# Hybrid HGRN2, short-convolution and MoE layer: a new order for the first tile and the masks, a product behind a later level, a conversion one turn sooner

## The chip, the cores and the metric

The kernel runs on one core of a Trainium2 chip. The metric is device time in microseconds (us) of one execution; the profile is of one further execution of the same program. TensorE is PE in all rows (PEld is its weight load), VectorE is DVE, ScalarE is ACT, GpSimd is POOL, and SP issues transfers.

## The reference, cut to what matters

There is one sequence of 1024 positions, 16 learned meta rows ahead of it, and 1024 channels.

```python
xn   = rmsnorm(h, norm_mix_g)                       # h: 1040 x 1024
proj = xn @ w_in                                    # q, f, i, g_out, B, C, v
# HGRN2, chunks of 128 tokens, 4 heads of 128x128 state:
o     = scores(q, k, decay) @ v + (q * exp(b)) @ state
state = exp(b_last) * state + (k * exp(b_last - b)).T @ v
h = h + concat(y_hgrn, y_conv) @ w_out
# top-8 of 64 experts, SwiGLU of width 256, in blocks of rows
h = h + moe_ffn(rmsnorm(h, norm_ffn_g), ...)
out = rmsnorm(h, norm_final_g)[16:]
```

## The kernel before

Three phases follow each other. `phase_front` holds the norm, the input projection, the HGRN2 chunks and the convolution, `phase_out_route` the output projection and the router, `phase_experts` the expert blocks and the last norm. Every engine has its own in-order program, and semaphores tie them. A product that must be precise is three matmuls: each operand is split into a high part (converted by ACT) and a low part (DVE subtracts the high part): high*high, high*low, low*high.

**First stage (0 to some 80 us).** The token tiles run through one pipeline of five steps. `root(c)` is Square with a sum, then Sqrt, on ACT; `recip` is on DVE; then ACT scales the rows (L582), PE turns the tile by 8 transposes (`turned(c)`, L379), DVE multiplies by the gain from PSUM (L778), ACT takes the high part (`high`, L548) and DVE the low part (`low`, L752). The order of tiles is `order`: the 16 meta rows first, then x0 to x7. `values(j)` (L368 to L370, 24 matmuls of 512 columns) multiplies tile j by the value columns `wi` of `w_in`. These 2 MB come in one transfer and are split in four pairs by ACT (L589) and DVE (L785), behind the third tile (`WI_AT = 2`). PE's program is turned(0), turned(1), turned(2), values(0), turned(3), values(1) and so on. POOL writes the constants and then fourteen `affine_select` masks (L286, L289); the masks are first read by the HGRN2 chunks. Behind the norm POOL starts the weight loop of the late columns (`load_late`, `store_late`: load a raw part, wait until ACT and DVE have split it, store the parts to DRAM).

**HGRN2 turns (182 to 447 us).** There are eight turns, one for each chunk, in pairs r = 0 and r = 1. PE's program mixes seven level products (`level(l)`, L465; level 0 is L457) with pieces of the late projections, which fill the time between levels (`BETWEEN`: three units of 512 columns from one level to the next). DVE prepares each level: `factors(l)` (L883, L884) multiplies the decays that ACT has exponentiated, `logs` (L876, L877) prepares a later level, `keep_scores` (L894) takes a level's scores over. After the diagonal scores (L906) stand three steps: `blast` (L910), QE = QE*QS (L911) and KE = KK*DK (L912, "end keys"). PE needs KE for a transpose behind level 6, and QE and all scores for the output product at the turn's end. POOL meanwhile works on the convolution, the last two of its products of a pair being L359.

**Experts (from some 750 us).** There are 65 items, one in each turn. Of each item the down matrix is split by ACT (`high_down`, L1783) and DVE (`low_down`, L1859), and then PE runs `down_rest` (L1722) and `down` (L1733 to L1735). ACT multiplies by the gates (L1802, L1806), and POOL adds the rows to `acc_rows` by two indirect transfers (`add_rows`, L1629 and L1633), after a wait until the previous item's adds have landed and two small index copies (L1624). When the last add has landed, SP loads the accumulated rows and the final norm runs.

## Time and profile before

| | |
|---|---|
| three runs | 1652.81, 1654.74, 1662.01 us, median 1654.74 |
| the profiled execution | 1652.65 us, of which the span from first to last instruction is 1651.1 |
| mean granted clock of TensorE | 0.981 of full |
| PE busy | 1562.9 us (95%), 10204 matmuls |
| DVE, ACT, POOL busy | 754.2, 654.2, 660.6 us |
| transfers | 375.17 MB, 227 GB/s over the span |

A row of the timeline has the start, the duration, the engine, the line, the operation with output and input names, how many instructions are merged in it, and in brackets how long the engine sat idle before it and what ended that. A wait row says which instruction waited for which, how long in total, how often, and the longest. On an engine that is busy without a gap, a shorter wait elsewhere changes nothing; a gap of PE that is removed moves all behind it.

### The profile page before, as it was taken

How to read it: one execution, taken by the hardware profiler on the slowest of the kernel's cores; microseconds unless marked ns; L12 is line 12 of the kernel's file. 1: busy time of each engine (PE TensorE's matmuls, PEld its weight loads, DVE VectorE, ACT ScalarE, POOL GpSimd, SP SyncE). 2: the span in 40 equal slices, each digit the busy share in tenths (PEclk: the TensorE clock that was granted, in tenths of full speed). 3: DMA queues.
4: the chain of work that ended last, by engine and by line, in shares of the span. 5: the costliest groups of instructions: out<-in, count | busy, mean ns of one | idle time of the engine just before them, and what ended most of it. 6: DMA issues, size and time to landing. Idle time of an engine off the chain costs nothing.

```text
span 1651.1 us, 30076 instructions
## 1 busy us (share of the span) xinstructions
PE 1562.9 (95%) x10204; PEld 1344.5 (81%) x10204; DVE 754.2 (46%) x1536; ACT 654.2 (40%) x1054; POOL 660.6 (40%) x825
## 2 busy tenths in 40 slices
PE   5999999999889999889999999999999999999991
PEld 4789989889644666679999999999999999999980
DVE  3323777788688774423333333333333333333333
ACT  7334544444433312024444444444444444444443
POOL 3022245162403232424545444555444445555531
PEclk9999999999999999989999999999999999999995
DMA  5389321211160112369999999999999999999977
GB/s 180 97 269 311 133 77 51 76 51 52 62 251 27 39 52 80 129 223 320 330 316 325 328 320 326 327 324 323 321 326 325 323 327 322 328 313 329 322 219 235
DMA packets 100728, 375.17 MB, mean 227 GB/s; under 512 B 14943, under 2 KB 31904, under 8 KB 79694
## 3 DMA queue, kind: packets, MB, share of 16 engines
q1 hardware_dynamic: 60606, 246.60, 40.9%
q0 software_dynamic: 40080, 128.04, 28.8%
q8 instruction: 23, 0.38, 0.1%
q14 instruction: 19, 0.16, 0.0%
HBM read 300.68 MB, written 73.91 MB: 227 GB/s over the span
## 4 chain that ended last, share of the span: by engine, by line
PE 54%; DMA 1%; ACT 0%; DVE 0%; issue 0%; SPq 0%; POOLq 0%; ACTq 0%
PE gu L1711 34%; PE ype L1733 4%; PE yrest L1722 4%; PE ype L1734 4%; PE ype L1735 4%; PE xp L1692 3%; PE xp L1699 1%; DMA A<-acc_rows 1%; DMA acc_rows<-YE,sia 0%; DVE WL L1859 0%; ACT WH L1783 0%; DVE A L1896 0%; SPq L1589 0%; ACT junkf L1846 0%; ACT XS L1787 0%
## 5 line engine op out<-in xcount | busy, mean ns | idle before, releaser
L1711 PE MATMUL gu<-XS,place 128*128 128x160 f32 x4160 | 588.2, 300 | 0.7 <-ACT XS L1791 0.7
L1711 PEld LDWEIGHTS gu<-XS,place 128*128 128x128 f32 x4160 | 575.6, 190 | 6.2 <-ACT XS L1791 1.1
L1859 DVE TENSOR_TENSOR WL<-place,WH 128x2048 fp32r<-128x2048 f32 x65 | 149.2, 2295 | 320.1 <-ACT WH L1783 320.1
L1796 ACT ACTIVATE SS<-gu 128x160 f32<-128x160 f32 x130 | 39.5, 304 | 367.0 <-PE gu L1711 367.0
L1864 DVE TENSOR_TENSOR SS<-SS,gu 128x160 f32<-128x160 f32 x130 | 41.3, 318 | 257.3 <-ACT SS L1796 257.3
L1806 ACT ACTIVATE YE<-ype,gta 128x512 f32<-128x512 f32 x130 | 89.5, 689 | 111.4 <-PE ype L1735 111.4
L1097 POOL DMA_INDIRECT slot_table<-pay,si x64 | 63.2, 988 | 172.3 <-DVEq L1396 155.2
L1629 POOL DMA_INDIRECT acc_rows<-YF,sib x65 | 104.3, 1604 | 64.9 <-POOL sib L1624 55.0
L1615 POOL COPY gta<-tables 128x1 f32 (+1 forms) x65 | 124.0, 1907 | 8.2 <-POOLq L952 8.2
L1783 ACT ACTIVATE WH<-place 128x2048 fp32r<-128x2048 f32 x65 | 123.5, 1900 | 0.7 <-issue 0.7
L1633 POOL DMA_INDIRECT acc_rows<-YE,sia x65 | 108.5, 1669 | 27.1 <-issue 22.5
L1733 PE MATMUL ype<-WH,hidh 128*128 128x512 f32 x260 | 110.0, 423 | 0.0
L1734 PE MATMUL ype<-WL,hidh 128*128 128x512 f32 x260 | 103.3, 397 | 0.0
L1735 PE MATMUL ype<-WH,hidr 128*128 128x512 f32 x260 | 101.9, 392 | 0.0
L1602 POOL DMA_INDIRECT wi<-xn_rows,gi x64 | 65.1, 1018 | 53.2 <-POOL gi L1599 52.1
L1624 POOL COPY sia<-tables 128x1 int32 (+1 forms) x65 | 11.9, 184 | 173.0 <-DMA acc_rows<-YE,sia 171.2
L1787 ACT COPY XS<-xp 128x512 f32<-128x512 f32 x130 | 69.8, 589 | 26.7 <-PE xp L1692 18.2
L1733 PEld LDWEIGHTS ype<-WH,hidh 128*128 128x128 f32 x260 | 49.1, 189 | 36.3 <-issue 27.2
L1722 PE MATMUL yrest<-place,HF 128*32 128x256 f32 x1040 | 70.5, 389 | 5.2 <-DVE WL L1859 5.2
L1692 PE MATMUL xp<-ident,wi 128*128 128x128 f32 x520 | 67.4, 273 | 2.3 <-PEq L952 2.3
L465 PEld LDWEIGHTS sc<-wi 128*128 128x128 f32 x448 | 56.8, 192 | 13.1 <-issue 8.7
L368 PE MATMUL bank<-xT_high,wf_parts 128*128 128x384 f32 (+2 forms) x192 | 67.2, 350 | 0.0
(311 smaller groups left out, 2850.5 us busy)
## 6 DMA issues: line engine op xcount, KB each, us to landing
place<-in_w_gate_e SPq DMA_DIRECT2D x65, 1024.0 KB
place<-in_w_up_e SPq DMA_DIRECT2D x65, 1024.0 KB
place<-in_w_down_e SPq DMA_DIRECT2D x65, 1024.0 KB
place<-in_w_in POOLq DMA_DIRECT2D x16, 512.0 KB, 6.9
late_parts<-wq_parts POOLq DMA_DIRECT2D x8, 1024.0 KB, 5.9
late_parts<-xn_parts POOLq DMA_DIRECT2D x8, 1024.0 KB, 6.1
wf_parts<-late_parts POOLq DMA_DIRECT2D x8, 1024.0 KB, 5.0
w_low<-late_parts POOLq DMA_DIRECT2D x8, 1024.0 KB, 5.1
```

What stands on the lines that cost most here:

```text
L1615: last = pool.tensor_copy(gt[q][r][:, :], K.gate[r][:, bass.ds(n, 1)])
L1629: pool.indirect_dma_start(acc_q, bass.IndirectOffsetOnAxis(ap=si[q][1][:, :], axis=0), YF[q][:, :], None, compute_op=ALU.add).then_inc(s_a ...
L1633: pool.indirect_dma_start(acc_d, bass.IndirectOffsetOnAxis(ap=si[q][0][:, :], axis=0), YE[q][:, :], None, compute_op=ALU.add).then_inc(s_a ...
L1692: last = pe.transpose(xp[t // 4][:, t % 4, :], rows[:, t, :], K.ident[:, :])
L1711: last = pe.matmul(gu[f][:, k, :], raw[:, t, f * P:f * P + P], XS[:, q, t, :], start=(t == 0), stop=(t == KT - 1))
L1722: last = pe.matmul(yr[j * CAP1:(j + 1) * CAP1, :], HF[q][:, f, P:CAP], raw[:, f, j * DQ:(j + 1) * DQ], start=(f == 0), stop=(f == 1), tile ...
L1733: pe.matmul(yp[g][:, :], hh, high[:, f, cols], start=(f == 0), stop=False)
L1734: pe.matmul(yp[g][:, :], hh, low[:, f, cols], start=False, stop=False)
L1735: last = pe.matmul(yp[g][:, :], hl, high[:, f, cols], start=False, stop=(f == 1))
L1783: act.activation(WH[q][:, :], WR[q][2][:, :], ACT.Copy).then_inc(s_dhi, 1)
L1806: act.activation(YE[q][:, 512 * g:512 * g + 512], yp[g][:, :], ACT.Copy, scale=gt[q][0][:, 0:1]).then_inc(s_ya, 1)
L1859: tt(WL[q][:, :], WR[q][2][:, :], WH[q][:, :].bitcast(F32), ALU.subtract).then_inc(s_dlo, 1)
```

## The change

1. SP loads x0, the gain and the meta rows, then `wi` in two halves with a semaphore each, then x1 to x7.
2. The meta rows come last (`order = list(range(TT + 1))`). ACT runs one Sqrt on a constant before the first tile. It converts two pairs of `wi` behind tile 0's scaling and two behind tile 1's. PE runs `turned(1)` in the middle of `values(0)`, and later tiles are turned two ahead of the values, not three. DVE follows that order.
3. POOL's masks are written behind the norm, after the first two `load_late` and the blank rows.
4. In each HGRN2 turn KE is behind level l = 2, `blast` and QE at l = 6.
5. In `add_rows` the index copies stand ahead of the wait for the previous adds. The last item's `high_down` moves into the turn before it, behind that turn's first sigmoid.

The diff, cut:

```diff
-        order = [TT] + list(range(TT))
+        order = list(range(TT + 1))
@@ sync
+            load_x(0)
+            sp.dma_start(gmix[:, :], ...).then_inc(s_m, 16)
             sp.dma_start(xt[0:META, TT, :], ins["meta_tokens"]).then_inc(s_m, 16)
-            load_x(0)
-            load_x(1)
-            sp.dma_start(K.wi[:, :, :], w_in[:, :, COL_I:COL_I + HW]).then_inc(s_wi, 16)
-            for j in range(2, TT):
+            for k in range(2):
+                sp.dma_start(K.wi[:, 4 * k:4 * k + 4, :], ...).then_inc(s_wi[k], 16)
+            for j in range(1, TT):
                 load_x(j)
@@ tensor, values(j)
-                pe.wait_ge(s_lo, TT + 1 if j == TT else j + 2)
+                pe.wait_ge(s_lo, j + 1)
...
+                    if j == 0 and t == KT // 2 - 1:
+                        turned(1)
...
-            for c in range(3):
-                turned(c)
+            turned(0)
             for j in range(TT):
                 values(j)
-                if j + 3 <= TT:
-                    turned(j + 3)
+                if j + 2 <= TT:
+                    turned(j + 2)
@@ scalar
+            act.activation(rstd[:, TT + 1:TT + 2], K.eps[:, 0:1], ACT.Sqrt)
+            root(0)
+            scaled(0)
+            act.wait_ge(s_wi[0], 16)
+            values_high(0)
+            values_high(1)
+            high(0)
+            root(1)
+            scaled(1)
+            act.wait_ge(s_wi[1], 16)
+            values_high(2)
+            values_high(3)
+            root(2)
@@ vector, front
+            keep_turned(0)
+            values_low(0)
+            low(0)
+            recip(1)
+            values_low(1)
+            values_low(2)
+            keep_turned(1)
+            values_low(3)
+            recip(2)
@@ vector, turn
-                dve.wait_ge(s_ee, i + 2)
-                step(nc.vector.tensor_copy(blast...))
-                tt(QE[:, :, :], QE[:, :, :], QS[:, :, :], ALU.mult)
-                step(tt(KE[:, :, :], KK[:, :, :], DK[:, :, :], ALU.mult))
-                dve.sem_inc(s_ke, 1)
                 for l in range(1, NL):
...
+                    if l == 2:
+                        dve.wait_ge(s_ee, i + 2)
+                        step(tt(KE[:, :, :], KK[:, :, :], DK[:, :, :], ALU.mult))
+                        dve.sem_inc(s_ke, 1)
+                    if l == NL - 1:
+                        step(nc.vector.tensor_copy(blast...))
+                        tt(QE[:, :, :], QE[:, :, :], QS[:, :, :], ALU.mult)
@@ gpsimd, add_rows
+                for r in two:
+                    pool.tensor_copy(si[q][r][:, :], ...).then_inc(s_si, 1)
                 if not isinstance(n, int) or n > 0:
                     pool.wait_ge(s_ad, n * 32)
                     pool.sem_inc(s_free, 1)
-                for r in two:
-                    pool.tensor_copy(si[q][r][:, :], ...).then_inc(s_si, 1)
@@ scalar, experts, turn_
-                high_down(q, n, i + 1)
                 if ahead >= 1:
+                    high_down(q, n, i + 1)
                     sigmoid(0, n + 1)
+                if ahead == 1:
+                    high_down(1 - q, n + 1, i + 2)
```

ACT's queue from the start of the program. Before (`place` holds the token tiles, `xT_high` the turned tile's high part; 16x1024 is the meta tile):

```order
L538 ACT_TABLE_LOAD
L538 ACTIVATE place,ss<-place 16x1024
L541 ACT_TABLE_LOAD
L541 ACTIVATE rstd<-ss,eps 16x1
L538 ACTIVATE place,ss<-place 128x1024
L541 ACTIVATE rstd<-ss,eps 128x1
L582 ACTIVATE place<-place,rstd 16x1024
L538 ACTIVATE place,ss<-place 128x1024
```

The same queue in the change, from its start to the first high part:

```order
L587 ACT_TABLE_LOAD
L587 ACTIVATE rstd<-eps 128x1
L538 ACTIVATE place,ss<-place 128x1024
L541 ACTIVATE rstd<-ss,eps 128x1
L579 ACTIVATE place<-place,rstd 128x1024
L584 ACTIVATE wi_high<-wi 128x1024 x2
L548 ACTIVATE xT_high<-xn 128x8x128
```

The meta tile and one table load have left the head of the queue, and half of the value weights stands between tile 0's scaling and its high part, where all four pairs stood behind tile 1's high part.

DVE's queue in an HGRN2 turn, from the diagonal scores on. Before:

```order
L906 TENSOR_TENSOR SCT<-sc,ident 128x512
L50 REGISTER_ALU
L909 REGISTER_ALU
L910 COPY blast<-place 128x4
L50 REGISTER_ALU
L911 TENSOR_TENSOR place<-place 128x512
L912 TENSOR_TENSOR place<-place 128x512
L50 REGISTER_ALU
L882 REGISTER_ALU
L883 TENSOR_TENSOR wi<-wi,place 128x8x32
L884 TENSOR_TENSOR wi<-wi,place 128x8x32
```

In the change, from the same place:

```order
L934 TENSOR_TENSOR SCT<-sc,ident 128x512
L50 REGISTER_ALU
L910 REGISTER_ALU
L911 TENSOR_TENSOR wi<-wi,place 128x8x32
L912 TENSOR_TENSOR wi<-wi,place 128x8x32
L904 TENSOR_TENSOR wi<-place 128x32x8
L905 TENSOR_TENSOR wi<-place 128x32x8
L917 REGISTER_ALU
L922 COPY_PREDICATED SCT<-masks,sc 128x4x64
```

The factors of the next level (8x32) now follow the diagonal scores at once; the end keys' product stands behind the level after it.

ACT's queue at the end of the experts, from the last but one turn's down matrix. Before:

```order
L1783 ACTIVATE WH<-place 128x2048
L1796 ACTIVATE SS<-gu 128x160 x2
L1802 ACTIVATE YF<-yrest,gtb 128x256
L1805 REGISTER_ALU
L1806 ACTIVATE YE<-ype,gta 128x512
L1805 REGISTER_ALU
L1806 ACTIVATE YE<-ype,gta 128x512
L1781 ISA
L1782 REGISTER_ALU
L1783 ACTIVATE WH<-place 128x2048
```

In the change:

```order
L1813 ACTIVATE WH<-place 128x2048
L1826 ACTIVATE SS<-gu 128x160
L1812 REGISTER_ALU
L1813 ACTIVATE WH<-place 128x2048
L1826 ACTIVATE SS<-gu 128x160
L1832 ACTIVATE YF<-yrest,gtb 128x256
```

The last item's conversion stands between the two sigmoids, ahead of the previous item's three evictions.

## Rows read from the trace of the kernel before

**Rows 1.** Waits of PE, whole span: total, times, longest.

```profile
PE sc L465 <- DVE wi L884: 8.8, 5, 2.2
```

**Rows 2.** Timeline of the first 35 us, ACT, DVE and PE.

```profile
11.07 1.13 ACT L582 ACTIVATE place<-place,rstd 128x1024 f32<-128x1024 f32 x1
...
14.26 0.69 DVE L778 TENSOR_TENSOR xn<-kt_ps,gmix 128x512 f32<-128x512 f32 x1 [1.54 <-PE o_ps L379]
14.38 1.06 ACT L538 ACTIVATE place<-place 128x1024 f32<-128x1024 f32 x1 [1.98 <-DMA place<-in_x]
...
15.89 0.16 DVE L745 RECIPROCAL rstd<-rstd 128x1 f32<-128x1 f32 x1 [0.34 <-ACT rstd L541]
...
16.95 1.97 PE L379 MATMUL sc<-ident,place 128*128 128x128 f32 x8 [2.73 <-ACT place L582]
17.75 3.88 ACT L589 ACTIVATE wi_high<-wi 128x1024 fp32r<-128x1024 f32 x4
...
20.22 4.62 DVE L785 TENSOR_TENSOR wi_low<-wi,wi_high 128x1024 fp32r<-128x1024 f32 x4
...
21.58 0.77 PE L368 MATMUL bank<-wi_high,xT_high 128*128 128x512 f32 x1 [2.65 <-DVE wi_low L785]
...
29.34 0.48 PE L368 MATMUL bank<-wi_high,xT_high 128*128 128x512 f32 x1
...
34.98 1.06 PE L379 MATMUL sc<-ident,place 128*128 128x128 f32 x8
```

**Rows 3.** Transfers: size, us from issue to landing; x0's issue, then wi's.

```profile
place<-in_x SPq DMA_DIRECT2D x1, 512.0 KB, 3.3
...
wi<-in_w_in SPq DMA_DIRECT2D x1, 2048.0 KB, 10.2
```

**Rows 4.** POOL busy while it writes the masks, 2 to 17 us.

```profile
2.00:17.00 15.00, 14.36 (x17) 1.00 0.94 355
```

**Rows 5.** Timeline: the first store of the late parts, and the third conversion.

```profile
84.33 0.59 POOL L304 DMA_DIRECT2D late_parts<-wq_parts  x1 [17.31 <-DVE wq_parts L764]
...
96.14 1.06 ACT L571 ACTIVATE wq_parts<-place 128x1024 fp32r<-128x1024 f32 x1
```

**Rows 6.** Timeline of the second turn of a pair, DVE, POOL and PE.

```profile
219.75 0.68 DVE L906 TENSOR_TENSOR SCT<-sc,ident 128x512 f32<-128x512 f32 x1
...
221.38 2.99 POOL L359 TENSOR_TENSOR place<-place 128x512 f32<-128x512 f32 x2
221.39 1.87 DVE L912 TENSOR_TENSOR place<-place 128x512 f32<-128x512 f32 x1
...
225.12 1.38 PE L465 MATMUL sc<-wi 128*128 128x64 f32 x8 [2.16 <-DVE wi L884]
```

**Rows 7.** Stretch of two us behind that wait: all engines, then granted clock.

```profile
226.00:228.00 2.00, 2.00 (x7) 1.71 (x7) 1.53 (x6) 0.00 (x0) 0.00 (x0) 0.50 0.00 0
```

**Rows 8.** Timeline of the last items: SP's issues, ACT, DVE, PE and POOL.

```profile
1579.02 13.66 SPq L1566 DMA_DIRECT2D place<-in_w_down_e  x2
...
1599.40 0.30 ACT L1796 ACTIVATE SS<-gu 128x160 f32<-128x160 f32 x1 [1.86 <-PE gu L1711]
...
1605.17 0.29 DVE L1870 TENSOR_TENSOR hidr<-HF,hidh 128x128 fp32r<-128x128 f32 x1
...
1608.28 1.90 ACT L1783 ACTIVATE WH<-place 128x2048 fp32r<-128x2048 f32 x1
...
1610.21 2.29 DVE L1859 TENSOR_TENSOR WL<-place,WH 128x2048 fp32r<-128x2048 f32 x1 [4.75 <-ACT WH L1783]
...
1612.84 1.93 PE L1722 MATMUL yrest<-place,HF 128*32 128x256 f32 x16 [5.18 <-DVE WL L1859]
...
1615.99 0.19 POOL L1624 COPY sia<-tables 128x1 int32 x1 [5.18 <-DMA acc_rows<-YE,sia]
...
1617.25 1.57 POOL L1629 DMA_INDIRECT acc_rows<-YF,sib  x1 [0.95 <-POOL sib L1624]
```

**Rows 9.** Chain that ended last, in order of time: start, us, step.

```profile
1620.95 6.12 DMA acc_rows<-YE,sia
```

More of the change, by code:

```diff
@@ L177, in phase_front @@
         s_x = [sem(f"x_in{j}") for j in range(4)]
-        s_m, s_wi = sem("meta_and_gmix_in"), sem("wi_in")
+        s_m, s_wi = sem("meta_and_gmix_in"), [sem(f"wi_in{i}") for i in range(2)]
         s_c0, s_c = sem("consts_cleared"), sem("consts_set")
@@ L571, in late_high, with scaled @@
                 act.activation(duo[k % 2][:, 0, :], raws[k % 2], ACT.Copy).then_inc(s_ph, 1)
-            act.wait_ge(s_c, 3)
-            root(0)
-            for c in range(TT + 1):
-                if c < TT:
-                    root(c + 1)
+            def scaled(c):
                 j, n = order[c], rows_of(c)
```

82 lines of the change are left out of this document (42 added, 40 removed).

## The prediction

> **What bounds the kernel now.** I read the busy shares first: PE is busy for 95% of the span, so only its gaps and what lies behind its last matmul can be won. The waits of PE show which gaps touch this change. Five waits on DVE's factors in the HGRN2 turns sum to 8.8 us [rows 1]; one of 2.65 stands before the first value product and one of 5.18 before the last item's down product [rows 2, 8]. Between the value products and the turns the timeline shows PE without a gap, so what is won in the first stage reaches the turns whole, if the queues beside PE keep up. The end is different: the last add of rows starts at 1620.95 and takes 6.12 [rows 9], and all behind it (SP's loads, the last norm) is untouched. A gain at the end must come through that add.
>
> **Part 1, the first tile.** Before, value tile 1 starts at 29.34 and ends at 34.98 [rows 2], 5.64 us for 24 matmuls, 0.235 each. By 34.98 PE has turned the meta tile and x0 to x2 and has done values 0 and 1. I work out when it has done the same in the new order.
> - x0's transfer lands 3.3 us after its issue [rows 3]. It is now the first, issued at 1.0 (0.9 sooner), so it lands at 4.3. ACT's one table load is over by then: it needs only the constants of POOL. From the start of a Square to the end of the reciprocal are 15.89 + 0.16 - 14.38 = 1.67 us; scaling takes 1.13 and turning by a PE that has just begun 1.97 [rows 2]. So: reciprocal 6.0, scaled 7.2, turned 9.2, and with two gain products (0.69 each, overlapping) stored at 10.5.
> - The first half of `wi`: all 2 MB land in 10.2 us, with x0 and x1 ahead [rows 3]. With x0 alone ahead I estimate 8.0 for the first half, 10.5 for the second, 12.0 for x1. A pair costs ACT 3.88/4 = 0.97 and DVE 4.62/4 = 1.15 [rows 2]. ACT has two pairs by 10.0 and the high part of x0 by 11.6; DVE runs pair 0's low part to 11.7 and x0's to 12.9. Values 0 start at 13.0, not 21.58.
> - They don't run through. x1's norm starts at 12.0, is scaled at 14.9, and pairs 2 and 3 are high at 15.9 and 16.9. DVE: low pair 1 to 14.9, pair 2 to 17.1, then x1's gain products behind its turning (18.1 to 19.4), then pair 3 to 20.6. PE reaches pair 3 at 19.5, waits 1.1 and ends values 0 at 22.0. x2 is scaled only after the reciprocal behind pair 3 (ACT 20.8 to 21.9), its turning ends at 23.1, x1's high part at 23.0 and low part at 24.3: PE waits 1.2 more, runs values 1, and ends at 24.3 + 5.6 = 29.9.
>
> The meta tile's turning is still owed, half a us. Gain: 34.98 - 29.9 - 0.5 = **4.6**. After that a tile's chain within one values group is 1.3 + 1.06 + 1.15 and three hand-overs, some 4.4 of 5.64 us, so two tiles ahead is enough. Bounds: 2.2, if all of values 0 runs at the slow pace (24 x 0.1 more: a turning takes 1.97 at 16.95 and 1.06 at 34.98 [rows 2], so both paces exist here); 6.9, if both waits vanish.
>
> The table load: only 1.3 us lie on the old chain for each of two loads, and the new one lies beside x0's transfer. The Trainium skill, "ScalarE: Activation LUTs", section "What ACT_TABLE_LOAD costs", states about 2.66 us for each switch of sets, 1.38 of it a drain. By that the old chain would show a longer gap than it does, and the new load would end near 4.6, 0.3 behind x0's landing; the sum would be 4.3 in place of 4.6.
>
> **The masks.** They take POOL 14.4 us [rows 4]; nothing of the first stage reads them, so there they cost and give nothing. Now they stand between the blank rows (over at about 66, an estimate) and the first store of late parts. That store starts at 84.33, when DVE has the parts [rows 5]; moved 4.6 earlier it would want 79.7, and the masks end at 66.2 + 14.7 = 80.9. Queued behind are the store and the next raw load, about 1.3 us late. ACT wants that load at 96.14 - 4.6 = 91.5 [rows 5]; issued by 82.4 it is there at 89.4, if its 512 KB take 7 us, midway between 3.3 and 10.2 [rows 3]. Cost nothing, with 2 us of cover.
>
> **Part 2, the end keys.** In the second turn of each pair the diagonal scores end at 220.43. Then DVE runs blast, QE and KE, KE in 1.87 us since it stands against POOL's L359 [rows 6], and PE idles 2.16 before level 2. PE was ready at 225.12 - 2.16 = 222.96. In the new order the factors start at about 220.6 and end by 221.4, before level 2 is wanted, so this wait goes in all four second turns. They hold four of the five waits of rows 1, at 2.1 each 8.5 us; the fifth, 0.2, stands before the last level of all. Behind the first of them the granted clock is 0.50, the lower level (1.2 GHz), for two us and more [rows 7], after a PE that had idled 2.16: that costs 1.6 and goes too. What is late next: L359 lasts to 224.37 [rows 6] and now stands against the two logs. KE lost 1.2 to it, so I take 2.3 lost in all; scores and factors of level 3 are then over between 226.2 and 226.8, and PE, three units of 9 x 0.235 and a level further, wants them at 226.0. Wait 0.6. KE then adds 0.9 to the next round and QE 0.9 to the last, where DVE's round (3.1) is about PE's (3.0): another 0.4 in small waits. So 1.0 comes back in each of three turns. The fourth has no gate work in it and loses only 0.4 at its end, where QE stands before the last scores. Sum: 8.5 + 0.2 + 1.6 - 3.0 - 0.4 = **6.9**. Bounds: 3, if half of each wait comes back and the clock falls again; 10.3, if none does. PE's own wait for KE (behind level 6) has 10 us of cover. In the first turn of a pair PE waits for nothing and the sum of DVE's work is the same: nothing.
>
> The Trainium skill, "SBUF — State Buffer", section "SBUF: two separate sides", has the port pair of DVE and GpSimd as an exclusive lock: an operation with two SBUF inputs waits until the other's ends. KE's 1.87 agrees. By the lock each of L359's two products holds up one DVE instruction, which is the later end of my 226.2 to 226.8 and would make the sum 6.3.
>
> **Part 3, the end.** The last item's down matrix is issued by 1592.7, 7 us before its conversion can start at 1599.7, behind the sigmoid [rows 8]. ACT has it at 1601.6, before the second sigmoid. DVE subtracts behind its hidden products, from 1605.5 to 1607.8. PE ends the previous item at 1612.84 - 5.18 = 1607.7 and runs L1722 from 1608.1, not 1612.84 [rows 8]: 4.7 sooner, and at the fast pace. That does not reach the end. The last item's adds wait until the previous item's have landed, at 1615.99 [rows 8], and those are untouched. Today L1629 runs 1.26 behind that landing, the two copies in between, then L1633 waits for ACT until 1620.95 [rows 9]. Now ACT is done by 1613, the copies are made, L1629 starts at about 1616.6, takes 1.57, and L1633 starts at 1618.5, not 1620.95. I take 0.2 off, since a second add that starts sooner behind the first takes longer to land. Gain **2.2**. Bounds: 1.3 (L1629 where it is today, the landing 0.5 longer) and 2.9. In the other turns add_rows has slack and gives nothing.
>
> **Sum**, against the profiled execution: 1652.65 - 4.6 - 6.9 - 2.2 = 1638.9. It lies 2.1 below the median of three runs; I put the forecast between, at **1639.5**.
>
> **Rivals.**
> A. *The waits of the turns only move.* L359 meets the new order badly in each pair, and level 3 or 4 waits as level 2 did. For it: DVE's round is as long as PE's. Against it: DVE arrives 3 us earlier. Part 2 falls to 3: 1643.
> B. *PE runs slow in the first stage*, with short waits between short runs of matmuls. Part 1 falls to 2.2: 1642.
> C. *Something beside PE holds the turns' start in place.* DVE's split of the last late parts and their stores depend on PE's evictions, which speaks against it. Part 1 falls to 0: 1644.
> D. *Slower.* The masks on POOL run beside DVE's splits and stretch. KE's factor against POOL is 1.87/0.69 = 2.7; by that they'd take 39 us and end at 105, the raw load would land at 113, and ACT, in order, would hold PE's evictions from 91.5 on: PE loses about 17: 1639 + 17 = 1656. It decides from masks of 19 us (first wait); for slower by 0.5% they must take 44. Against it: they ran at their price beside DVE's splits of the first stage.
> E. *The early conversion does not run early*, the matrix not landed at 1599.7: if it holds the second sigmoid, which is due when PE ends its next product, part 3 is 0 or a loss of 2: 1641 to 1643.
>
> **How the numbers follow.** Forecast 0.60; A 0.16, B 0.08, C 0.07, D 0.03, E 0.06. The upper bounds of all parts together give 1632.6, the lower 1646.2. The range is 1634 to 1646.5. About 0.5% is what a measurement of this kernel can tell from no change, 8.3 us: faster needs 1646.5 or less. Same holds where two of A, B, C meet (0.09); slower is D (0.03); faster 0.88.
>
> **What would show it.** Values 0 start near 13 and values 1 end near 30, with two PE waits of about 1; the masks end near 81 and ACT's third conversion has no new wait; no PE wait of 2 us before level 2, no stretch at clock 0.50, small ones before level 3; L1722's last wait under 1 us, L1629 starting within a us of the landing, L1633 2 us sooner against the previous landing. I would be wrong most if x1's transfer lands after 14, or if the new waits in the turns exceed 1 us each.

## The result, and the profile of the changed kernel

| | before | after |
|---|---|---|
| median, this measurement | 1660.77 us (1652.81 to 1662.01, 5 runs) | 1643.35 us (1643.14 to 1645.78, 5 runs) |
| profiled execution, span | 1652.65 us, 1651.1 us | 1643.35 us, 1641.8 us |
| granted TensorE clock, mean of the span | 0.981 | 0.983 |

The ratio of the times is 0.9917, 95% interval 0.9895 to 0.9939. Measured twice more on other occasions, the changed kernel gave 0.9917 [0.9893, 0.9941] and 0.9928 [0.9906, 0.995]. So it is faster by 0.8%, and more than the 0.5% that can be told from no change. The forecast of 1639.5 was 3.9 us too low; the measured time lies inside the stated range. Between the two profiled executions 9.3 us were gained, where 13.7 were worked out.

Where PE waits now, longest first (PE's operation and line, what it waited for, us in total, times, longest); it answers to [rows 1]:

```profile
PE sc L378 <- ACT place L579: 7.8, 1, 7.8
PE xp L1722 <- PEq L982: 6.0, 1, 6.0
PE op L1167 <- DVE place L1362: 5.9, 1, 5.9
...
PE sc L465 <- DVE wi L912: 3.1, 6, 1.0
```

The factors' waits (`sc L465`) fell from 8.8 to 3.1 us. The second line has nothing to do with any edit: PE's own sequencer (PEq) waited 6.0 us at the barrier ahead of the experts, where all engines meet, and 2.3 in the kernel before.

The first stage, from the timelines (start, duration, engine, line, operation, idle before and what ended it), answers to [rows 2]; ACT, DVE and PE in the order of time:

```profile
1.03 1.28 ACT L587 ACT_TABLE_LOAD   x1 [1.03 <-PEq L1963]
2.33 0.20 ACT L587 ACTIVATE rstd<-eps 128x1 f32<-128x1 f32 x1
7.75 1.94 PE L378 MATMUL sc<-ident,place 128*128 128x128 f32 x8 [7.75 <-ACT place L579]
8.99 2.00 ACT L584 ACTIVATE wi_high<-wi 128x1024 fp32r<-128x1024 f32 x2 [1.38 <-DMA wi<-in_w_in]
12.22 1.23 DVE L767 TENSOR_TENSOR xT_low<-xn,xT_high 128x1024 fp32r<-128x1024 f32 x1
13.50 0.79 PE L367 MATMUL bank<-wi_high,xT_high 128*128 128x512 f32 x1 [3.81 <-DVE xT_low L767]
...
21.36 0.51 PE L367 MATMUL bank<-wi_high,xT_high 128*128 128x512 f32 x1 [1.11 <-DVE wi_low L796]
24.83 0.50 PE L367 MATMUL bank<-wi_high,xT_high 128*128 128x512 f32 x1 [0.90 <-DVE xT_low L767]
30.50 0.60 PE L378 MATMUL kt_ps<-ident,place 128*128 128x128 f32 x4
62.90 1.05 PE L378 MATMUL sc<-ident,place 16*128 16x16 f32 x8
```

Values 0 start at 13.50, values 1 end at 30.50 (34.98 before), and the meta tile's eight transposes cost 1.05 us at 62.90. Further on, three stretches are counted off by PE's first product of the turns, the first of the output stage behind them (`ms`) and the first expert product (`gu`):

```profile
179.17 1.15 PE L457 MATMUL sc<-place 128*128 128x128 f32 x8 [1.41 <-ACT place L694]
...
439.92 2.93 PE L1153 MATMUL ms<-place,ones 128*128 128x512 f32 x3 [2.87 <-ACT place L1286]
...
709.45 2.77 PE L1741 MATMUL gu<-XS,place 128*128 128x160 f32 x9 [0.74 <-ACT XS L1821]
```

In the kernel before the same three stand at 182.36, 449.64 and 716.40. So 3.2 us were won ahead of the turns; the turns took 260.75 in place of 267.28, 6.5 won; and the stretch from there to the experts took 269.5 in place of 266.8, 2.8 lost.

The end, which answers to [rows 8, 9] (PE's last down product and POOL's last two adds, from the timelines, and the landing, from the chain of waits):

```profile
1600.54 1.07 PE L1752 MATMUL yrest<-place,HF 128*32 128x256 f32 x16 [0.25 <-DVE WL L1891]
...
1609.34 1.57 POOL L1659 DMA_INDIRECT acc_rows<-YF,sib  x1 [5.44 <-issue]
1611.21 1.54 POOL L1663 DMA_INDIRECT acc_rows<-YE,sia  x1 [0.30 <-issue]
```

```profile
1611.21 6.52 DMA acc_rows<-YE,sia
```

The last add starts 14.94 us behind the down product of the item before it (at 1596.27), where it was 17.31 (1603.64 and 1620.95): 2.4 won. The landing took 6.52 for 6.12 and the experts 0.4 less, which cancel. Sum: 3.2 + 6.5 - 2.8 + 2.4 = 9.3, the whole difference of the two executions.

So three questions are open: is the loss of 2.8 ahead of the experts the change's doing; which edit carries what; and why do the times differ by more than the 9.3 of the two profiles? By the ratio it is 13.7; the two medians of five lie 17.4 apart, and the later sets, with 24 and 17 runs of the kernel before, give 13.6 and 12.4.

### The profile page after: what moved, and what is told of

Read it like the earlier page. It is cut to its first block, busy times and chain, and to the rows that moved or that the text cites. A ratio compares the mean times of both kernels' runs of the same rounds, so it can differ in the third digit from the quotient of the medians.

```text
span 1641.8 us, 30075 instructions
## 1 busy us (share of the span) xinstructions
PE 1557.7 (95%) x10204; PEld 1340.5 (82%) x10204; DVE 759.8 (46%) x1536; ACT 653.5 (40%) x1054; POOL 668.0 (41%) x825
## 4 chain that ended last, share of the span: by engine, by line
PE 54%; DMA 1%; DVE 1%; issue 0%; ACT 0%; POOL 0%; POOLq 0%; ACTq 0%; DVEq 0%; SPq 0%
PE gu L1741 35%; PE ype L1763 4%; PE yrest L1752 4%; PE ype L1764 4%; PE xp L1722 4%; PE ype L1765 3%; PE xp L1729 1%; DMA acc_rows<-YE,sia 1%; DVE A L1928 1%; DMA A<-acc_rows 0%; POOL acc_rows L1659 0%; DVE rtf L1926 0%; ACT XS L1821 0%; ACT XS L1817 0%; ACT YF L1832 0%
## 5 line engine op out<-in xcount | busy, mean ns | idle before, releaser
L1645 POOL COPY gta<-tables 128x1 f32 (+1 forms) x65 | 138.3, 2128 | 9.5 <-POOLq L982 9.5
L1663 POOL DMA_INDIRECT acc_rows<-YE,sia x65 | 103.3, 1589 | 30.7 <-issue 22.4
L1722 PE MATMUL xp<-ident,wi 128*128 128x128 f32 x520 | 68.3, 275 | 6.0 <-PEq L982 6.0
L1752 PE MATMUL yrest<-place,HF 128*32 128x256 f32 x1040 | 69.6, 385 | 0.2 <-DVE WL L1891 0.2
L1167 PE MATMUL op<-wo,place 128*128 128x512 f32 x128 | 59.9, 612 | 7.4 <-DVE place L1362 5.9
L1722 PEld LDWEIGHTS xp<-ident,wi 128*128 128x128 f32 x520 | 61.3, 142 | 6.8 <-issue 6.8
```

The source lines that it names most:

```text
L1645: last = pool.tensor_copy(gt[q][r][:, :], K.gate[r][:, bass.ds(n, 1)])
L1663: pool.indirect_dma_start(acc_d, bass.IndirectOffsetOnAxis(ap=si[q][0][:, :], axis=0), YE[q][:, :], None, compute_op=ALU.add).then_inc(s_a ...
L1722: last = pe.transpose(xp[t // 4][:, t % 4, :], rows[:, t, :], K.ident[:, :])
L1752: last = pe.matmul(yr[j * CAP1:(j + 1) * CAP1, :], HF[q][:, f, P:CAP], raw[:, f, j * DQ:(j + 1) * DQ], start=(f == 0), stop=(f == 1), tile ...
```

## Experiments

Twelve kernels ran, in three groups on one chip each, beside 24, 19 and 17 runs of the kernel before (medians 1654.45, 1655.45 and 1654.98). The ratios are against these.

### The parts, one at a time

`e0_after` is the changed kernel. `e1_front` has the first stage and the masks alone, `e2_keys` only the move of KE, `blast` and QE, `e3_end` only the early conversion and the index copies (diffs as shown in the section on the change).

> The whole change again, on the same chip as its parts. Theory S (the parts save time where they stand and the stretch from the output projection to the first expert item is a matter of chance): the first turn of HGRN2 starts 3.2 us sooner than before, the eight turns are 6.5 us shorter, the last add comes 2.4 us sooner against the last item but one; the stretch from the first matmul of the output phase (450 us before) to the first expert product varies by several us from profile to profile, for the kernel before too. Theory K (the change itself lengthens that stretch, since PE is later at the barrier between the phases): the wait of PE's sequencer before the first expert transposes is about 6.0 us here again and 2.3 in the kernel before.

> The first stage and the masks' place of the change alone. The first HGRN2 level product at 179.2, as in the whole change (182.4 before); the four waits of 2.1 us in the second turns stay; the end as before. Theory S: 3.3 us faster than before. Theory K: the sequencer's wait at the expert phase is longer than before only if this part causes it, and then the gain is near 0.

> The end keys' product and QE at later levels alone. First level product at 182.4 as before; the eight turns 6.5 us shorter (260.8 for 267.3 from the first level product to the first matmul of the output phase), waits at level 3 of 0.5 to 1.0 in place of 2.1 at level 2. Theory S: 6.5 us faster. Theory K: some 3 us less than that, if a sooner arrival at the phase barrier is what makes PE wait there.

> The last down matrix sooner and the index copies ahead of the wait, alone. Nothing changes before the last items. The last item's first product starts 4.8 us sooner, the last add 2.4 us sooner: 2.0 to 2.4 us faster by either theory. If the adds were not what bounds the end, it would be 4.8 or more.

| | median us | ratio [95%] | start of turns | turns | to the experts | sequencer's wait | last add behind the down product before |
|---|---|---|---|---|---|---|---|
| profile of before | | | 182.36 | 267.3 | 266.8 | 2.3 | 17.3 |
| e0_after | 1640.85 | 0.9917 [0.9893, 0.9941] | 179.89 | 260.75 | 265.5 | 2.9 | 15.05 |
| e1_front | 1650.76 | 0.9979 [0.9964, 0.9995] | 179.87 | 267.3 | 267.1 | 5.0 | 17.1 |
| e2_keys | 1644.59 | 0.9942 [0.9922, 0.9962] | 182.67 | 260.75 | 265.5 | 5.0 | 16.2 |
| e3_end | 1652.69 | 0.9990 [0.9970, 1.0009] | 182.94 | 272.0 | 267.5 | 5.0 | 15.1 |

Theory K, that the change itself lengthens the sequencer's wait, falls: with one edit alone, and any of them, the wait is 5.0, and the changed kernel has 6.0 in one profile, 2.9 in the second and 2.3 in a third. The stretch to the experts varies from 264 to 269.5 over all profiles of this study. The 2.8 us were chance.

What PE waits for there can be read from the barrier's own steps. GpSimd's step, DRAIN, in the changed kernel's profile (duration in ns, then its start in us), and then in `e11_after`, the same kernel:

```profile
L982 POOLq DRAIN  x1: 11717/11717/11717, 692.8 to 692.8; - x1
```

```profile
L982 POOLq DRAIN  x1: 9273/9273/9273, 692.0 to 692.0; - x1
```

It starts at 692.75 and ends at 704.47, and PE's next product starts at 704.91. In 11 of the 14 profiles PE starts 0.44 us behind the end of this step, and in the other three (before, `e9_scores_first`, `e11_after`) 0.42 behind SP's last step at the barrier. So the wait is 2.3 us where GpSimd is done in time, and up to 6.2 where it isn't; its DRAIN took 9.3 to 12.0 us. Why its length varies is open.

Each part gains where it stands: the front starts the turns 2.5 to 3.2 sooner, the end keys take 6.5 off the turns, the end 2.2. But by the medians the end keys alone gain 9.9, and `e3_end`, which doesn't touch the turns, took 272.0 for them. Its waits are those of the kernel before. What differs is the clock behind them. The windows of `e3_end` behind its second wait (window, its length, busy times of PE, PEld, DVE, ACT, POOL with instructions, granted clock, DMA share, GB/s), and then the same from `e1_front` behind the only one of its four with a fall:

```profile
295.00:296.00 1.00, 0.54 (x3) 0.55 (x3) 1.00 (x4) 0.00 (x0) 0.00 (x0) 0.74 0.51 197
296.00:298.00 2.00, 2.00 (x9) 1.90 (x9) 1.53 (x6) 0.00 (x0) 0.00 (x0) 0.50 0.00 0
298.00:300.00 2.00, 2.00 (x6) 1.52 (x6) 1.03 (x4) 1.00 (x2) 0.00 (x0) 0.50 0.00 0
300.00:302.00 2.00, 2.00 (x9) 1.71 (x7) 0.49 (x2) 1.36 (x3) 0.00 (x0) 0.50 0.00 0
302.00:303.00 1.00, 1.00 (x7) 0.96 (x7) 1.00 (x4) 0.25 (x1) 0.00 (x0) 0.85 0.00 0
```

```profile
222.00:223.00 1.00, 0.37 (x3) 0.38 (x3) 1.00 (x4) 0.00 (x0) 0.00 (x0) 0.92 0.67 262
223.00:224.00 1.00, 1.00 (x7) 1.00 (x6) 0.74 (x3) 0.00 (x0) 0.00 (x0) 0.50 0.00 0
224.00:225.00 1.00, 1.00 (x4) 0.90 (x5) 0.78 (x3) 0.00 (x0) 0.00 (x0) 0.50 0.00 0
225.00:226.00 1.00, 1.00 (x3) 0.74 (x3) 1.00 (x4) 0.01 (x1) 0.00 (x0) 0.50 0.00 0
226.00:227.00 1.00, 1.00 (x5) 0.85 (x4) 0.20 (x1) 1.00 (x2) 0.00 (x0) 0.87 0.00 0
```

In both the clock is at its lower level, 1.2 GHz, behind a wait of PE of 2.14 and 2.16 us; for 3.4 us in `e1_front`, for 6.8 in this place of `e3_end`. `e3_end` has two more stretches of 3.4. Summed over the turns, the part of the clock that is missing comes to 1.7 us in `e1_front` and in the profile of before, and to 6.8 in `e3_end`: the turns' 267.3 and 272.0 follow from it. `e2_keys`, with waits of 0.96, has this behind its first one:

```profile
227.00:229.00 2.00, 1.86 (x12) 1.74 (x13) 1.73 (x5) 1.74 (x3) 0.00 (x0) 1.00 0.00 0
```

This is theory C of the runs that follow: each wait of 2.1 us may bring a stretch at the lower clock, by chance, and the waits of 1 us don't.

### The masks' place

`e4_masks_first` is the changed kernel with this undone:

```diff
+            pool.memset(masks[:, :, :], 1).then_inc(s_cst0, 1)
+            for l, half in enumerate(LEVELS):
...
             pool.wait_ge(s_tr, TT + 1)
...
             pool.memset(fill[:, :, 1:2], 0.0).then_inc(s_blank, 1)
-            pool.memset(masks[:, :, :], 1).then_inc(s_cst0, 1)
-            for l, half in enumerate(LEVELS):
...
```

> The whole change, but POOL builds the masks at the start, as in the kernel before. In the changed kernel the masks end at 82.74 and DVE's four small operations and its split beside them are stretched (0.79, 1.57, 0.52 and 1.92 us, where the kernel before has 0.16, 0.16, 0.17 and 1.23). Theory M (the masks' place costs and gives nothing): here the small operations take 0.2 each again, the split 1.2 us, the first store of late parts is issued at about 81 in place of 84.1, and nothing behind it moves: first level product at 179.2 to 179.9, time within 2 us of the changed kernel. Rival (DVE's stretched split is on PE's path, or the masks beside the first stage slow x0's chain): the first level product moves by over 1 us, down to 176 or up to 182.

Median 1642.25 us (1639.62 to 1643.58), ratio 0.9922 [0.9901, 0.9944]. Theory M is half wrong: the first level product came at 180.38, later than the 179.2 to 179.9 expected, and not by the 1 us of the rival. DVE in `e4_masks_first`, x0's low part and two pairs of the value weights:

```profile
11.97 1.93 DVE L767 TENSOR_TENSOR xT_low<-xn,xT_high 128x1024 fp32r<-128x1024 f32 x1
...
14.37 2.06 DVE L796 TENSOR_TENSOR wi_low<-wi,wi_high 128x1024 fp32r<-128x1024 f32 x1
16.61 2.32 DVE L796 TENSOR_TENSOR wi_low<-wi,wi_high 128x1024 fp32r<-128x1024 f32 x1 [0.19 <-ACT wi_high L584]
```

POOL's last two masks beside them:

```profile
13.06 2.83 POOL L285 TENSOR_SCALAR_AFFINE_SELECT masks<-masks 128x256 int16<-128x256 int16 x1
15.96 2.44 POOL L288 TENSOR_SCALAR_AFFINE_SELECT masks<-masks 128x256 int16<-128x256 int16 x1
```

DVE's three take 1.2 each in the changed kernel, and POOL's two 2.12 each: here both engines are held up, the fourteen masks by 1.6 us in sum (14.52 for 12.91 from the first select to the end of the last). From the start of x0's turning to values 0 PE needs 6.46 us here, and 5.75 to 5.77 in seven profiles with the masks late. (An eighth has 6.18, but there the weights landed half a us later.) The two stretched pairs have cover: from x1's turning to x3's both kernels need 12.7. So the masks' move is worth 0.7 us at the front. Behind it nothing moves: from x3's turning to the first level product it takes 148.9 us with the masks first and 148.4 to 149.1 with them late.

In their new place they stretch other work. DVE and then POOL in the changed kernel, around the first store of late parts:

```profile
77.43 0.79 DVE L823 TENSOR_TENSOR place<-place 128x4 f32<-128x4 f32 x1 [8.46 <-ACT place L615]
...
78.46 1.57 DVE L825 TENSOR_TENSOR place<-place 128x4 f32<-128x4 f32 x1
80.06 0.52 DVE L826 TENSOR_SCALAR place<-place 128x4 f32<-128x4 f32 x1
81.36 1.92 DVE L779 TENSOR_TENSOR wq_parts<-place,wq_parts 128x1024 fp32r<-128x1024 f32 x1 [0.78 <-DVE place L826]
```

```profile
80.62 2.12 POOL L308 TENSOR_SCALAR_AFFINE_SELECT masks<-masks 128x256 int16<-128x256 int16 x1
84.08 0.58 POOL L289 DMA_DIRECT2D late_parts<-wq_parts  x1 [1.34 <-DVE wq_parts L779]
```

With the masks first the four take 0.16, 0.16, 0.17 and 1.23, and the store is issued at 81.98. The Trainium skill, "SBUF — State Buffer", section "SBUF: two separate sides", has the port pair of DVE and GpSimd as an exclusive lock. The rows agree in part. In the changed kernel only DVE is held up: the masks take 14.6 us from the first to the last instruction here and 14.7 before, and DVE's instructions start while a select runs (77.22 to 78.48, 78.44 to 80.56, 80.62 to 82.74) and wait no longer than it lasts. With the masks first both sides are held up, as the select of 2.83 above shows. But DVE's first two (77.43, 78.46) end 0.3 and 0.5 us ahead of the select's end, and the split ends 0.54 behind it, though it needs 1.23 alone; so the rows do not show a hold to the very end of a select. The late masks cost nothing here: the raw load behind the store is issued at 84.74 and lands at 91.31, and ACT's conversion of it starts at 92.83. That is a cover of 1.5 us; in `e4_masks_first` the load lands at 89.34 for a conversion at 93.80.

### One pair sooner

`e7_low3` is the changed kernel with

```diff
-            keep_turned(1)
             values_low(3)
+            keep_turned(1)
             recip(2)
```

> The changed kernel, but DVE makes the low part of the fourth pair of the value matrix ahead of x1's two gain products instead of behind them. In the changed kernel PE waits 1.11 us for that pair (18.85 to 21.36 holds only six matmuls) and then 0.90 for x1's low part. Expected: DVE has pair 3 at 19.1, the gain products run 19.1 to 20.4, the first wait goes, the second becomes 1.0 to 1.2, values 1 end at 29.6 in place of 30.50, the first level product is 0.8 to 0.9 sooner. Rival (x1's high part and x2's scaling on ACT get later by as much): the second wait grows by 1 and nothing is won. Either lies below what the median time can tell (0.05%), so it is read from the trace.

PE in `e7_low3`, x1's turning, the first product of values 1, and x3's turning:

```profile
18.12 0.60 PE L378 MATMUL kt_ps<-ident,place 128*128 128x128 f32 x4
...
24.02 0.50 PE L367 MATMUL bank<-wi_high,xT_high 128*128 128x512 f32 x1 [1.06 <-DVE xT_low L767]
...
29.68 0.60 PE L378 MATMUL kt_ps<-ident,place 128*128 128x128 f32 x4
```

The wait of 1.11 is gone, the second is 1.06, and from x1's turning to x3's PE needs 11.56 in place of 12.70: 1.1 us won, where 0.8 to 0.9 were expected. Median 1638.41 us (1637.07 to 1641.79), ratio 0.9904 [0.9882, 0.9926], against 1642.25 of `e4_masks_first` beside it. The gain of 1.1 is read from the trace; the medians, of kernels that differ in the masks too, are too coarse to show it. So in the prediction's own account of values 0 one of the two waits was avoidable by moving one line.

### What is late at level 3

`e8_short_gate` is the changed kernel with POOL's gate product cut to 8 tokens of each half, so its outputs are not the reference's:

```diff
-                    tokens = slice(k * half, k * half + half)
+                    tokens = slice(k * half, k * half + 8)
                     step(pool.tensor_tensor(y[:, tokens], y[:, tokens], B[:, tokens], ALU.mult))
```

> The changed kernel, with POOL's product of the convolution's output with its gate cut to 8 of 512 tokens in each of its two instructions (the outputs are therefore not the reference's). In the changed kernel this product (2.72 us for the two) stands against DVE's logs 904 and 905 of the second turns, which take 1.95 and 1.50 where they take 0.42 alone, and PE waits 0.96 before level 3. Theory L (that contention is the wait): the logs take 0.42 to 0.6, the waits before level 3 go in all four second turns (3 us in sum), the small waits of 0.2 and 0.3 may stay; the stretch from the first level product to the last stage's first product is 257.8 in place of 260.75. Rival (the clamp and the hand-overs ahead of the factors are the wait): 0.5 us or more stays before level 3 in each.

`e9_scores_first` is the changed kernel with

```diff
                 for l in range(1, NL):
-                    factors(l)
+                    if l != 2:
+                        factors(l)
+                    if l == 1:
+                        keep_scores(0)
+                        factors(2)
                     if l + 2 < NL:
                         logs(l + 2)
-                    keep_scores(l - 1)
+                    if l > 1:
+                        keep_scores(l - 1)
```

> The changed kernel, but in each turn of the recurrence DVE does level 1's scores and level 3's factors ahead of level 4's logs instead of behind them. In the changed kernel those two logs stand against POOL's gate product in the second turns (1.95 and 1.50 us where they take 0.42), and level 3's factors, for which PE waits 0.96, stand behind them. Theory Q (what matters is what is queued behind the contention, not the contention): the scores and factors now meet the gate product and are over by 221.3 of the changed kernel's trace, the logs run later alone, the waits before level 3 go in the first three second turns, the small ones of the last pair (0.2 to 0.3) stay, and the recurrence takes 257.5 to 258.5 us from the first level product to the last stage's first product in place of 260.75; median 2 to 3 us below the changed kernel. Rival R (the delay only moves on): the clamp, ACT's two steps behind it and the decays of level 4 get later, and PE waits 0.6 to 1.0 before level 4 instead; 260 to 261 as before.

In the changed kernel POOL's gate product meets the two logs, and PE waits for the factors queued behind them. POOL, DVE and PE of the changed kernel:

```profile
218.46 2.72 POOL L358 TENSOR_TENSOR place<-place 128x512 f32<-128x512 f32 x2
```

```profile
218.10 1.95 DVE L904 TENSOR_TENSOR wi<-place 128x256 f32<-128x256 f32 x1
219.97 1.50 DVE L905 TENSOR_TENSOR wi<-place 128x256 f32<-128x256 f32 x1
...
223.07 0.42 DVE L912 TENSOR_TENSOR wi<-wi,place 128x256 f32<-128x256 f32 x1
```

```profile
223.62 1.10 PE L465 MATMUL sc<-wi 128*128 128x64 f32 x8 [0.96 <-DVE wi L912]
```

In `e8_short_gate` the logs take 0.41 and 0.42, and none of the first three second turns has a wait before level 3. The turns take 256.15 us against 260.75, 4.6 less where 3 were expected. Compared product by product, the difference falls at the five waits that are gone: 0.96, 0.96, 0.17, 0.52 and 0.23 long, they are worth 1.2, 1.3, 0.5, 0.8 and 0.6. So a wait costs 0.2 to 0.3 more than its length, of which 0.1 is the level product behind it (1.10 in place of 1.00). 0.24 stays before the last level of the last turn. The whole is slower (1662.35, ratio 1.0046), because with products missing tokens go to other experts and there are 67 items in place of 65; that says nothing of the gate product.

In `e9_scores_first` the contention stays and meets other instructions:

```profile
218.30 1.98 DVE L912 TENSOR_TENSOR wi<-wi,place 128x256 f32<-128x256 f32 x1
...
221.61 0.41 DVE L912 TENSOR_TENSOR wi<-wi,place 128x256 f32<-128x256 f32 x1
```

Level 3's factors are over at 222.0 in place of 223.5 and its product waits for nothing. The turns take 258.2 us, 2.6 less, and no new wait over 0.3 appears before level 4: theory Q held and R fell. Median 1639.55 us, 3.1 below the changed kernel beside it (`e11_after`, 1642.61).

### The two edits of the end

`e5_down` is the kernel before with the early conversion alone, `e6_copies` with the two index copies alone.

> The kernel before with the early conversion of the last down matrix alone, without the move of the two index copies. Theory S (the last add is bound by the landing of the previous item's adds): PE's down product of the last item comes 5 us sooner behind the last product before it, a wait under 0.5 in place of 5.18; the first of the last two adds still starts 1.2 us behind the landing (two copies in between) and the second 1.8 to 1.9 behind the first: the last add is 1.7 to 1.9 sooner than before against the start of the last item, 0.5 less than with both edits. Rival (each edit needs the other): the last add gains nothing or all 2.4. In the turns of the recurrence (unchanged here) four waits of 2.0 to 2.2 us stay; theory C (TensorE's granted clock falls behind some of them, by chance) expects between one and three stretches of 2 us or more under 0.8 of the full clock behind them, and a time for those turns of 267 with one and 272 with three; a fall in none would speak against it. Median time 1 to 4 below the kernel before.

> The kernel before with the two index copies of POOL ahead of its wait for the previous item's adds, and nothing else. In the kernel before the second of the last item's adds waits 2.13 for ACT's rows, so the copies are not what it stands on. Theory S: the first of the last two adds starts about 0.9 sooner against the item before, the second still waits for ACT and the last add starts no sooner (within 0.3, if the clock behind PE's wait of 5.18 is the same); median within 1 us of the kernel before. Rival (the copies carry the end's gain): the last add comes 1 us sooner or more. In the recurrence four waits of 2.0 to 2.2; theory C expects one to three of them with a stretch at half clock of 3.4 us or more behind it.

POOL in `e5_down`, then in `e6_copies`, from the previous item's last add on:

```profile
1620.81 0.18 POOL L1624 COPY sia<-tables 128x1 int32 x1 [5.18 <-DMA acc_rows<-YE,sia]
...
1622.07 1.57 POOL L1629 DMA_INDIRECT acc_rows<-YF,sib  x1 [0.95 <-POOL sib L1624]
1623.94 1.54 POOL L1633 DMA_INDIRECT acc_rows<-YE,sia  x1 [0.30 <-issue]
```

```profile
1620.41 1.57 POOL L1629 DMA_INDIRECT acc_rows<-YF,sib  x1 [3.96 <-issue]
1623.51 1.54 POOL L1633 DMA_INDIRECT acc_rows<-YE,sia  x1 [1.54 <-ACT YE L1806]
```

Behind the down product of the item before, the last add starts 15.6 us later with the conversion alone, 16.1 with the copies alone, 15.1 with both, and 16.2 to 17.3 with neither. The early conversion takes the last add off ACT's rows and onto the landing of the adds before, and the copies give 0.5 to 0.7 on top of it, but by themselves nothing: their last add still waits for ACT. Where neither is there the spread of 1.1 follows the clock behind PE's wait of 5.18: low for 6.8 us with 17.3 and 17.1, for under 4 with 16.2. Medians 1653.38 (ratio 0.9992 [0.9976, 1.0008]) and 1650.95 (0.9984 [0.9969, 1.0]): too little to be told apart from the kernel before. For `e6_copies` a median within 1 us of the kernel before was expected, and it lies 4.0 below; its trace, of an execution of 1655.57, shows no cause.

### The clock, and the best version

`e11_after` is the changed kernel again. `e10_both` has the edits of `e7_low3` and `e9_scores_first` together.

> The changed kernel once more, as the measure for the kernels beside it, and for the spread. Theory C (the kernel before is spread over 10 us because each of its four waits of 2.1 us may bring a stretch of TensorE at half clock, and the changed kernel has none of these): waits in the recurrence of 0.96 or less, no second at the lower clock between the first level product and the last stage; the times of all runs within 5 us of each other, against 10 for the kernel before. One stretch at the lower clock in the recurrence would speak against it.

> The changed kernel with the value matrix's fourth low part ahead of x1's gain products (0.84 us sooner at the end of values 1, in the earlier run) and with the scores and factors ahead of the logs (as in the run beside this one). Theory Q: the two add: values 1 end at 29.7, the recurrence takes 257.5 to 258.5, and the median lies 3 to 4 us below the changed kernel's. Rival R: 0.8 us below it and no more.

Theory C, over all profiles: the four waits of 2.0 to 2.2 us stand in the turns of five profiles (before, `e1_front`, `e3_end`, `e5_down`, `e6_copies`).

| profile | waits of 2.0 to 2.2 with a lower clock behind | clock missing in the turns, us | turns, us |
|---|---|---|---|
| before | 1 of 4 | 1.7 | 267.3 |
| e1_front | 1 of 4 | 1.7 | 267.3 |
| e5_down | 2 of 4 | 3.4 | 268.9 |
| e6_copies | 2 of 4 | 3.4 | 268.9 |
| e3_end | 3 of 4 | 6.8 | 272.0 |
| nine profiles with waits of 1.0 or less | none | 0 | 256.2 to 260.9 |

So 9 of 20 such waits brought a fall, and none of the shorter ones did. It is no even draw: the first of the four waits had one in all five profiles, the second in three, the third in one and the fourth (2.02 to 2.05 long) in none. What sets this is open. The turns follow the missing clock: without it they are 265.2 to 265.6 in all five. On average 3.4 us are missing, twice what the one profile of before shows.

The runs that were not profiled say the same, since each has its mean granted clock on record. Over 60 runs of the kernel before, the time follows the clock that is missing in the whole run (correlation 0.96, 1.03 us for each us), and 32.1 us are missing on average; over 17 runs of the changed kernel it is 28.7, so 3.5 less.

That answers the third question. Averaged over the profiles, the front gives 3.1, the turns 8.1 and the end 1.8 (15.0 for 16.8 behind the down product before), 13.0 in all, where the two medians with many runs of the kernel before give 13.6 and 12.4. The pair of profiles shows only 9.3, since before's was a fast one (1652.65 for a mean of 1654.2 over the 60 runs) and after's a slow one (1643.35 for 1642.2 over 17).

The spread narrows, as theory C expected: 2.6 to 4.9 us in each set of 5 or 6 runs of the changed kernel, 3.9 in `e2_keys`, and 9.2 in the set of 5 runs of the kernel before (10.3 to 10.8 in its sets of 17 to 24).

`e10_both` gave 1636.94 us (1634.83 to 1639.44, 6 runs), ratio 0.9897 [0.9875, 0.9919], and `e11_after` beside it 1642.61 (1639.81 to 1643.83). No run of the one reaches into the other's: 5.7 us less, where 3 to 4 were expected of theory Q; the traces account for 3.7, and the rest is not explained. In its profile the turns take 258.2 us and x1's turning to x3's 11.57, the two gains as they were alone. It is faster than both the kernel before and the changed one.

## Why the prediction came out as it did

**What bounds the kernel**: right. PE is busy for 95% of the span, and the gains are those of its gaps.

**Part 1, 4.6 forecast, 3.2 in the profile of after.** Over all profiles the turns start at 182.7 on average with the old front (five, 182.4 to 183.0) and at 179.6 with the new one as it stands (six, 179.2 to 179.9): 3.1. Its chain holds, with each hand-over where it was put, but these terms were mis-sized, and they are where the sum of this part failed:
- The first half of `wi` was put at 8.0 and was there at 8.99 (8.6 to 9.5 in others). With x0 scaled 0.4 late this carries to values 0, 13.50 for 13.0.
- In values 0 PE waited 1.11 for pair 3 (forecast 1.1), and 0.90 before values 1 (forecast 1.2), and ended them at 30.50 for 29.9. So 0.6 is owed to the start.
- The meta tile's turning was put at half a us. Its eight transposes of 16 rows take 1.05, as much as eight of 128 rows (1.06). In the kernel before they lay in PE's idle time; now they are on the path. 0.5 more.
- The masks were said to cost and to give nothing in the first stage. They gave 0.7 (`e4_masks_first`). The sum held this without saying so, since it priced DVE's pairs by the row at 20.22, behind the masks' end at 16.9 [rows 2, 4].
- The rest, 0.2 to 0.3, lies between there and the turns; 0.1 of it is the wait before their first product (1.0 to 1.9 long in the fourteen profiles).

**The masks behind the norm**: cost 0, right, and the cover was thinner than said. They ended at 82.74 for 80.9, since POOL began them at 68.1 and not 66.2, and they stretched DVE's split, so that the first store came at 84.08 for 81. The raw load landed at 91.31 with 1.5 us of cover, where 89.4 and 2 were forecast. Rival D's mechanism exists: in this place it holds up DVE, by 3.1 us in sum, and not POOL, and with the masks first it holds up POOL too, by 1.6 (`e4_masks_first`). The argument against it was a misreading: the masks of the kernel before end at 16.9 and its splits start at 20.22 [rows 2, 4], so they had not met.

**Part 2, 6.9 forecast, 6.5 in the profile and 8.1 on average** (turns of 268.9 in five profiles, 260.8 without the waits). The four waits went, at 2.1 each; the first factors met their level; the residual before level 3 was put at 0.6 and was 0.96, 0.96, and 0.17 with 0.52 in three turns; the later small ones, put at 0.4 a turn, did not come in the first two. 3.0 forecast to come back, 2.6 came; the last turn 0.8 for 0.4 (0.23 and 0.26 before its levels, 0.32 before the output product). Its cause is the one named, L359's contention: without it the waits are gone. The step that failed in this part is the clock. The prediction priced the one fall in the profile, 1.6, as if it were all that the kernel loses. Falls came behind 9 of 20 such waits and are worth 3.4 on average, so the part is worth 1.7 more than one profile shows. That the profile's 6.5 is so near 6.9 is in part luck: a wait costs 0.2 to 0.3 more than its length, which no term has, and the waits that came back cost that too. Rival A was true in its mechanism, since the wait moved to level 3, but it fell by its size, 2.6 in place of half.

**Part 3, 2.2 forecast, 2.4 in the profile, 2.2 in e3_end.** Near by its number, and right by its steps: L1752 (L1722 before) waits 0.25 in place of 5.18, the first add starts when the adds before have landed, and the second 1.87 behind it. Rival E fell. The landing of the last add went from 6.12 us to 6.52, where 0.2 were taken off for it; in the other profiles it is 5.98 to 6.23 with the second add 1.9 behind the first and 6.25 to 6.39 with 2.5 to 3.5, so the reason given for the 0.2 has no support beyond the one profile of before. What the sum left out is that the clock behind the wait of 5.18 sets when PE's products, and so ACT's rows, are ready: in the profiles the gain is 1.1 to 2.4, 1.8 on average.

**The sum.** 13.7 forecast, 12.1 by the parts where they stand, and 9.3 between the two profiled executions. Two steps failed. Of the 4.4 us between 13.7 and 9.3 (the other two parts come to 0.2 together), 1.4 are part 1, by the terms above (the first half of `wi` at 8.99 for 8.0, the meta tile at 1.05 for 0.5), and 2.8 lie in a stretch that no edit touches and that the sum put at nothing. There PE's sequencer waited 6.0 us at the barrier before the experts and not 2.3, behind GpSimd's DRAIN of 11.7 us. The forecast measured its sum against one execution as if all but its own terms would stand still, and in this kernel two of them don't: this wait (2.3 to 6.2) and the falls of the clock. The prediction's range took in the bounds of the edits, 1632.6 to 1646.2, and not these; that it held the time all the same is partly luck, as the falls of the clock were worth 1.7 more than it said and the barrier cost 2.8.

**Rival C** fell: nothing beside PE holds the turns' start. `e1_front` alone starts them 2.5 sooner.

## What to carry to other kernels

Price a wait on TensorE by more than its length: it cost 0.2 to 0.3 more here, and behind one of 2 us the clock may fall. One profile shows only one case of that, so a kernel with several such waits should be read in several profiles. When a contention between two engines can't be avoided, look at what is queued behind it: moving the work that PE waits for ahead of the logs gave 2.6 us at no cost, although the contention stayed. Work that is read by nobody near it isn't free on POOL: its place decides which DVE instructions are stretched. And before a forecast is measured against one profile, look at what in it belongs to no edit: a wait at a barrier can be several us longer in the next.

## What the runs showed of the hardware

- Eight transposes of 16 rows take 1.05 us on TensorE, eight of 128 rows 1.05 to 1.06.
- In the turns the granted clock fell to the lower level (1.2 GHz) behind 9 of 20 waits of 2.0 to 2.2 us, for 3.4 us mostly and once for 6.8, and behind none of 0.97 or less. In the fourteen profiles it was at that level within 1.5 us behind the wait of 2.87 in the next stage in twelve, and behind that of 5.92 in all, in eight of them from before this wait on.
- At the program's start products of 512 columns start 0.43 us apart, the lower level, up to the first clock record, and 0.23 apart from there on.
- POOL's selects on 16-bit masks and DVE's instructions hold up each other: DVE's went from 0.16 us to 0.79 and 1.57 for four elements a partition and from 1.23 to 1.92, 2.06 and 2.32 for 1024; POOL's from 2.12 to 2.83 and 2.44 where DVE was at work beside them in the first stage.
- PE's sequencer waits 2.3 to 6.2 us at the barrier ahead of the experts, in kernels that are the same up to it, and three profiles of one kernel have 6.0, 2.9 and 2.3. In 11 of 14 profiles the wait ends with GpSimd's DRAIN, of 9.3 to 12.0 us.
